# High-half products ahead of low-half products in every weight tile of a two-block fp32 network

## The reference

```
def reference(x, ...):
    x = first_block(x, ...)      # 2 layers: in-projection, mLSTM heads, retention heads, gates,
                                 # out-projection, feed-forward 1024-4096-1024, gated embedding
    return second_block(x, ...)  # layer 0: GLA + RWKV mixer, layer 1: attention with an index;
                                 # behind each a product-key expert layer with 16384 experts
...
z = h @ w_in[i] + b_in[i]
x = x + jnp.square(jax.nn.relu(h2 @ w_ff1[i] + b_ff1[i])) @ w_ff2[i] + b_ff2[i]
```

## Time and profile before

| what | value |
|---|---|
| median of 3 runs | 3336.14 us (3334.34 to 3337.27) |
| profiled execution, its own time | 3334.71 us |
| its span, first to last instruction | 3332.9 us |
| TensorE busy | 3222.9 us (97%) |
| VectorE busy | 2154.8 us (65%) |
| ScalarE busy | 1498.9 us (45%) |
| GpSimd busy | 506.1 us (15%) |
| DMA, mean | 170 GB/s |
| mean granted TensorE clock | 0.993 |

### The profile page before, as it was taken

How to read it: one execution, slowest core, us unless ns; L and a number is a source line. 1 busy time by engine, 2 the same in 40 slices (tenths; PEclk the granted TensorE clock), 3 DMA queues, 4 the chain that set the end, 5 groups by cost and what they waited for, 6 DMA issues and landing times.

```text
span 3332.9 us, 49471 instructions
## 1 busy us (share of the span) xinstructions
PE 3222.9 (97%) x20642; PEld 2851.4 (86%) x20642; DVE 2154.8 (65%) x3111; ACT 1498.9 (45%) x1717; POOL 506.1 (15%) x278
## 2 busy tenths in 40 slices
PE   8999999999999999989999999999999999999998
PEld 7787789787877897877999989888769999989887
DVE  6765665577666555685887755555677967655555
ACT  6444454564444544612444444444344444444443
POOL 0000000000000000010766600000003766300000
PEclk9999999999999999999999999999999999999999
DMA  5454645444545454303444465555424444565553
GB/s 222 149 184 165 214 165 188 166 152 163 182 169 207 173 183 166 146 18 112 175 167 149 152 234 199 189 189 193 173 89 152 166 164 152 198 220 182 197 190 126
DMA packets 87656, 565.12 MB, mean 170 GB/s; under 512 B 10192, under 2 KB 10208, under 8 KB 23568
## 3 DMA queue, kind: packets, MB, share of 16 engines
q1 hardware_dynamic: 80496, 534.81, 44.8%
q0 software_dynamic: 6944, 27.21, 2.5%
HBM read 552.54 MB, written 9.44 MB: 169 GB/s over the span
## 4 chain that ended last, share of the span: by engine, by line
PE 52%; DVE 5%; ACT 2%; issue 1%; POOL 1%; DVEq 0%; ACTq 0%
PE bank L1981 7%; PE bank L1982 7%; PE bank L1983 7%; PE bank L2004 7%; PE bank L2003 7%; PE bank L2002 7%; PE bank L1964 3%; ACT w_hi L2128 1%; PE bank L1713 1%; PE bank L1689 1%; PE bank L1691 1%; PE bank L1690 1%; PE bank L1715 1%; PE bank L1714 1%; POOL w_lo L1613 1%
## 5 line engine op out<-in xcount | busy, mean ns | idle before, releaser
L2128 ACT ACTIVATE w_hi<-raw 128x2048 fp32r<-128x2048 f32 x291 | 557.5, 1916 | 763.8 <-PE bank L2004 377.2
L2405 DVE TENSOR_TENSOR w_lo<-raw,w_hi 128x2048 fp32r<-128x2048 f32 x222 | 509.7, 2297 | 564.3 <-ACT w_hi L2128 563.6
L974 DVE TENSOR_TENSOR w_lo<-raw,w_hi 128x2048 fp32r<-128x2048 f32 x200 | 458.1, 2292 | 358.8 <-ACT w_hi L735 357.3
L735 ACT ACTIVATE w_hi<-raw 128x2048 fp32r<-128x2048 f32 x201 | 384.6, 1915 | 483.9 <-PE bank L489 330.7
L1981 PE MATMUL bank<-act_hi,w_hi 128*128 128x256 f32 x2048 | 591.9, 289 | 5.1 <-POOL w_lo L1613 5.1
L1983 PE MATMUL bank<-act_hi,w_lo 128*128 128x256 f32 x2048 | 580.2, 283 | 0.0
L1982 PE MATMUL bank<-act_lo,w_hi 128*128 128x256 f32 x2048 | 580.0, 283 | 0.0
L2004 PE MATMUL bank<-w_hi,c_lo 128*128 128x512 f32 x1024 | 399.5, 390 | 0.0
L2003 PE MATMUL bank<-w_lo,c_hi 128*128 128x512 f32 x1024 | 399.2, 390 | 0.0
L2002 PE MATMUL bank<-w_hi,c_hi 128*128 128x512 f32 x1024 | 399.0, 390 | 0.0
L1981 PEld LDWEIGHTS bank<-act_hi,w_hi 128*128 128x128 f32 x2048 | 392.9, 192 | 6.5 <-POOL w_lo L1613 6.3
(11 more groups left out here) (507 smaller groups left out, 5693.4 us busy)
## 6 DMA issues: line engine op xcount, KB each, us to landing
raw<-weights SPq DMA_DIRECT2D x492, 1024.0 KB, 4.8
row<-rows POOLq DMA_DIRECT2D x48, 256.0 KB, 4.3
spill<-staged SPq DMA_DIRECT2D x32, 256.0 KB, 2.9
hid<-spill SPq DMA_DIRECT2D x32, 256.0 KB, 4.8
y<-w_pe POOLq DMA_DIRECT2D x2, 1024.0 KB, 5.0
ln_row_mix<-ln_rows POOLq DMA_DIRECT2D x4, 512.0 KB, 4.9
hid<-keys POOLq DMA_DIRECT2D x2, 1024.0 KB, 6.2
ln_row_ffn<-ln_rows POOLq DMA_DIRECT2D x4, 512.0 KB, 7.7
```

What stands on the lines that cost most here:

```text
L735: nc.scalar.activation(w_hi[:, k % SPLIT, :], raw[:, k % RAW, :], ACT.Copy).then_inc(hi_ready, 1)
L974: nc.vector.tensor_tensor(w_lo[:, k % SPLIT, :], raw[:, k % RAW, :], w_hi[:, k % SPLIT, :].bitcast(F32), ALU.subtract).then_inc(lo_ready, 1)
L2128: A.activation(hi_of(k), raw[:, k % RAW, :], ACT.Copy).then_inc(hi_ready, 1)
L2405: V.tensor_tensor(lo_of(k), raw[:, k % RAW, :], hi_of(k).bitcast(F32), ALU.subtract).then_inc(lo_ready, 1)
```

## The change

In every weight tile TensorE waits for `hi_ready` first, issues all products with `w_hi` (high x high and low x high), then waits for the low half, and issues the products with `w_lo`. The number of products, their operands, and the place of `tile_used` at the tile's end stay. In the token-half form each half has its own high group and low group. In `hidden`, `gates` is called behind the same counts of products as before. The waits for activations (`ready`, `halves_of`) stand in the high group.

```
@@ first block, TensorE @@
+            def mm2(dst, lh, ll, rh, first):
+                nc.tensor.matmul(dst, lh, rh, start=first, stop=False)
+                nc.tensor.matmul(dst, ll, rh, start=False, stop=False)
...
             def natural(...):
                 for j in range(per) if tiles is None else tiles:
                     k = k0 + j
-                    pe.wait_ge(lo_ready, base + (k + 1))
+                    pe.wait_ge(hi_ready, base + (k + 1))
                     apart = half is not None and j == per - 1
-                    for kk, t in [... t outer] if apart else [... kk outer]:
-                        ...
-                        last = mm3(psum[2 * (c % 2) + t][:, :], hi[:, ki, ts], lo[:, ki, ts], w_hi[:, k % SPLIT, ws],
-                                   w_lo[:, k % SPLIT, ws], ki == 0, ki == per * KB - 1)
-                        if apart and t == 0 and kk == KB - 1:
+                    for group in [(t,) for t in range(TT)] if apart else [tuple(range(TT))]:
+                        for kk in range(KB):
+                            ki, ws = j * KB + kk, slice(kk * CW, (kk + 1) * CW)
+                            if ready is not None and 0 in group:
+                                ready(j, kk)
+                            for t in group:
+                                ts = slice(t * P, (t + 1) * P)
+                                mm2(psum[2 * (c % 2) + t][:, :], hi[:, ki, ts], lo[:, ki, ts], w_hi[:, k % SPLIT, ws], ki == 0)
+                        pe.wait_ge(lo_ready, base + (k + 1))
+                        for kk in range(KB):
+                            ki, ws = j * KB + kk, slice(kk * CW, (kk + 1) * CW)
+                            for t in group:
+                                last = nc.tensor.matmul(psum[2 * (c % 2) + t][:, :], hi[:, ki, t * P:(t + 1) * P], w_lo[:, k % SPLIT, ws],
+                                                        start=False, stop=ki == per * KB - 1)
+                        if apart and 0 in group:
                             last.then_inc(half, 1)
                     last.then_inc(tile_used, 1)
...
             def featured(...):   # both blocks alike; order is (f, kk) or (kk, f) in the first
-                    pe.wait_ge(lo_ready, base + (k + 1))
+                    pe.wait_ge(hi_ready, base + (k + 1))
+                    for kk, f in order:
+                        ...      # ready(j, kk) where f == 0, then w_hi x act_hi and w_hi x act_lo
+                    pe.wait_ge(lo_ready, base + (k + 1))
+                    for kk, f in order:
+                        ...      # w_lo x act_hi
                     last.then_inc(tile_used, 1)
@@ second block, hidden @@
-                wait_lo(pe, k)
+                pe.wait_ge(hi_ready, k + 1)
...
+                def product(of, jj, by, **marks):
+                    nonlocal done
+                    ws = slice((2 * kk_ + jj) * P, (2 * kk_ + jj + 1) * P)
+                    ins = mm(psum[4 + p % 2][:, jj * S:(jj + 1) * S], of[:, ws], by[:, kk_, :], **marks)
+                    done += 1
+                    if done == 3 * UNITS:
+                        ins.then_inc(tile_used, 1)
+                    if done % 3 == 0 and done // 3 - 1 in after:
+                        gates(after[done // 3 - 1])
                 for jj in range(2):
                     for kk_ in range(KD):
+                        product(wh, jj, act_hi, start=kk_ == 0 and jj == 0, stop=False)
+                        product(wh, jj, act_lo, start=False, stop=False)
+                wait_lo(pe, k)
+                for jj in range(2):
+                    for kk_ in range(KD):
+                        product(wl, jj, act_hi, start=False, stop=kk_ == KD - 1 and jj == 1)
@@ second block, output @@
-                wait_lo(pe, k)
+                pe.wait_ge(hi_ready, k + 1)
                 pe.wait_ge(c_lo_ready, p0 + o + 1)
+                for group in [(t,) for t in range(TT)] if end else [tuple(range(TT))]:
+                    parts = [(t, jj, c) for t in group for jj in range(2) for c in range(2)]
+                    ...          # for each part: c_hi x wh, c_lo x wh
+                    wait_lo(pe, k)
+                    ...          # for each part: c_hi x wl
```

More of the change, by code:

```diff
@@ L1680, in natural @@
                 k = k0 + j
-                wait_lo(pe, k)
+                pe.wait_ge(hi_ready, k + 1)
                 apart = half is not None and j == 1
[L1683 to L1692, removed]
+                for group in [(t,) for t in range(TT)] if apart else [tuple(range(TT))]:
+                    for kk_ in range(KB):
+                        ki, ws = j * KB + kk_, slice(kk_ * CW, (kk_ + 1) * CW)
+                        if 0 in group:
+                            halves_of(ki, split)
+                        for t in group:
+                            dst = psum[2 * (c % 2) + t][:, :]
+                            mm(dst, act_hi[:, ki, HALVES[t]], w_hi[:, k % SPLIT, ws], start=ki == 0, stop=False)
+                            mm(dst, act_lo[:, ki, HALVES[t]], w_hi[:, k % SPLIT, ws], start=False, stop=False)
+                    wait_lo(pe, k)
+                    for kk_ in range(KB):
+                        ki, ws = j * KB + kk_, slice(kk_ * CW, (kk_ + 1) * CW)
+                        for t in group:
+                            last = mm(psum[2 * (c % 2) + t][:, :], act_hi[:, ki, HALVES[t]], w_lo[:, k % SPLIT, ws], start=False, stop=ki == KD - 1)
+                    if apart and 0 in group:
                         last.then_inc(half, 1)
@@ L1710, in featured @@
                         dst = psum[2 * (c % 2) + f // 2][:, (f % 2) * S:(f % 2 + 1) * S]
[L1711 to L1715, removed]
+                        mm(dst, w_hi[:, k % SPLIT, ws], act_hi[:, ki, :], start=ki == 0 and f % 2 == 0, stop=False)
+                        mm(dst, w_hi[:, k % SPLIT, ws], act_lo[:, ki, :], start=False, stop=False)
+                wait_lo(pe, k)
+                for f in range(4):
+                    for kk_ in range(KB):
+                        ki = j * KB + kk_
+                        ws = slice(kk_ * CW + f * P, kk_ * CW + (f + 1) * P)
+                        dst = psum[2 * (c % 2) + f // 2][:, (f % 2) * S:(f % 2 + 1) * S]
+                        last = mm(dst, w_lo[:, k % SPLIT, ws], act_hi[:, ki, :], start=False, stop=ki == KD - 1 and f % 2 == 1)
                 last.then_inc(tile_used, 1)
@@ L1976, in hidden @@
                 after = dict(GROUPS_IN.get(p, ()))
+                done = 0
+                def product(of, jj, by, **marks):
[7 more added lines that the diff above has]
+                        gates(after[done // 3 - 1])
                 for jj in range(2):
-                    dst = psum[4 + p % 2][:, jj * S:(jj + 1) * S]
                     for kk_ in range(KD):
[L1980 to L1988, removed]
+                        product(wh, jj, act_hi, start=kk_ == 0 and jj == 0, stop=False)
+                        product(wh, jj, act_lo, start=False, stop=False)
+                wait_lo(pe, k)
+                for jj in range(2):
+                    for kk_ in range(KD):
+                        product(wl, jj, act_hi, start=False, stop=kk_ == KD - 1 and jj == 1)
             def output(o):
@@ L1993, in output @@
                 begin, end = o == 0, o == EXPERT_PAIRS - 1
-                wait_lo(pe, k)
+                pe.wait_ge(hi_ready, k + 1)
                 pe.wait_ge(c_lo_ready, p0 + o + 1)
                 wh, wl = hi_of(k), lo_of(k)
[L1997 to L2005, removed]
+                for group in [(t,) for t in range(TT)] if end else [tuple(range(TT))]:
+                    parts = [(t, jj, c) for t in group for jj in range(2) for c in range(2)]
+                    for t, jj, c in parts:
+                        cs, ws = slice(jj * S + t * P, jj * S + (t + 1) * P), slice(jj * D + c * CW, jj * D + (c + 1) * CW)
+                        mm(psum[2 * t + c][:, :], c_hi[:, o % 2, cs], wh[:, ws], start=begin and jj == 0, stop=False)
+                        mm(psum[2 * t + c][:, :], c_lo[:, o % 2, cs], wh[:, ws], start=False, stop=False)
+                    wait_lo(pe, k)
+                    for t, jj, c in parts:
+                        cs, ws = slice(jj * S + t * P, jj * S + (t + 1) * P), slice(jj * D + c * CW, jj * D + (c + 1) * CW)
+                        last = mm(psum[2 * t + c][:, :], c_hi[:, o % 2, cs], wl[:, ws], start=False, stop=end and jj == 1)
+                    if end and 0 in group:
                         last.then_inc(half_done, 1)
```

20 lines of the change are left out of this document (7 added, 13 removed).

## The result

The kernel with the change takes 3316.01 us (median of 4 runs, 3314.81 to 3319.13) against 3336.7 us for the kernel before (4 runs, 3334.34 to 3341.45): ratio 0.9932, 95% interval 0.992 to 0.9945. It is faster by 0.7%, 20.7 us by the medians, where 22.2 us were forecast. The profiled execution took 3319.13 us, with a span of 3317.3 us.

A forecast was written before the change was run, and what follows sets the result against it. TensorE works for 97% of the span, so only its 110 us of idle time and what slows its stream can be won. 24.6 - 0.7 - 1.7 = 22.2 us less gives 3313.5 us, range 3304 to 3327.

The forecast's parts named there:

- How large one stall is: TensorE's waits for w_lo: each costs its idle time + 0.25 us, since the idle column understates it.
- Removed, the first block: First block: 17 stalls for w_lo give 16.0 us, five tile starts too short for the idle column 1.9 us.
- Not kept: Three stalls per first-block layer and one in the second block: 6.7 us, counted at nothing, as TensorE then waits for VectorE.
- rival 2: All is kept: VectorE's chains also begin earlier, 6.7 us on top, and the clock costs nothing: 3305.5 us; chance 0.08.
- GpSimd's w_lo, "they are kept": Expert stage, three stalls per layer: 6.7 us stay gained; the nearest chain, the selection, has 5.4 us slack against 3.4 gained.
- What it adds, a fulfilled wait and bank changes: Some 500 mid-tile waits taken as 0 (outer end 40 us); bank switches of 2272 low products taken 0 (bound 23 us).
- Fresh activations: Second block's feature-major chunks: activations still being split are consumed faster, 0.24 us new wait three times, 0.7 us lost.
- The clock: First block, transposes: longer second wait may bring a 3.4 us stretch at 1.2 GHz in both layers; 1.7 us lost.
- more than two stretches beyond those of before: Sign of being wrong: more than two stretches at 1.2 GHz beyond those of the kernel before.
- 1 (half of the first block's gain lost): VectorE's chains turn half of the first block's 17.9 us into longer waits: gain 13 us, 3323 us; chance 0.20.
- 3 (slower by the wait): Mid-tile wait breaks the overlap of weight loads and products, 0.08 us per tile, net +18 us: 3354 us; chance 0.05.
- 4 (nothing): Nothing measurable: the high half isn't really early, or the gain is given back where weights stream; chance 0.05.

The follow-up runs named there:

- c_after: The kernel after, unaltered, run again as the mark for the follow-up edits to VectorE's and GpSimd's work: 3315.28 us, ratio 0.9933 to the kernel before.
- e6_y: Kernel after with VectorE's gatings put ahead of low splits (one in the mLSTM section, two in retention), so y is ready sooner: 3306.79 us, ratio 0.9911.
- e5_sel: Kernel after with the low half of the expert layers' tile 24 written by VectorE behind the selection instead of by GpSimd: 3310.95 us, ratio 0.9922.
- e3_order: New order of products in every tile, but TensorE waits for the low half at the tile's top as in the kernel before: 3338.92 us, ratio 1.0004.
- e4_waits: Kernel after plus about 5600 more fulfilled waits, one behind every pair of high products: 3313.24 us, ratio 0.9923 to the kernel before.
- c_after2: The kernel after, unaltered, run once more as the mark in a later group: 3315.47 us, ratio 0.9929 to the kernel before.
- e1_first: Kernel before with the new order and late wait in the first block only: 3316.48 us, ratio 0.9933.
- e7_both: Kernel after with both VectorE's earlier gatings of y and tile 24's low half moved from GpSimd to VectorE: 3305.08 us, ratio 0.9901.

## Why the prediction was right, step by step

Where the time went is read from the starts of the 492 `w_hi` in the profiles of before and c_after, whose spans differ by 3332.9 - 3314.8 = 18.1 us:

| part | forecast us | found us |
|---|---|---|
| first block, stalls kept | -17.9 | -18.3 |
| GpSimd's w_lo, kept | -6.7 | -6.6 |
| seven stalls not kept (y, keys) | 0 | 0 |
| selection late, both layers | 0 | +4.0 |
| granted clock in the first block | +1.7 | +5.6 - 3.2 = +2.4 |
| fresh activations, and what is left over | +0.7 | +0.4 |

The last row is what closes the sum. It holds steps of 1 to 1.5 us of both signs, and the larger ones lie at the clock: near 1395 us 1.5 us are lost where the granted clock is 0.50 for 6.8 us in c_after (from 1370.2) and for 3.4 us in before (from 1386.5), near 1420 and 2475 us 1.1 and 1.5 us are won the other way round (6.8 us at 0.50 in before, 3.4 in c_after), and near 2512 us 1.5 us are lost beside 3.4 us at 0.50 (from 2493.2) that before lacks.

**How large one stall is: right.** At the boundary of the earlier trace rows the gain is 1.20 us where the column said 0.98 and idle + 0.25 says 1.23. GpSimd's three in the first expert layer gave 1.26, 0.87 and 1.21 us, 3.33 us in all, and those of the second 3.30, against the 3.36 counted.

**Removed, the first block: right.** The sum over both layers is 9.2 + 9.1 us. The smallest, among them the five too short for the idle column, gave 0.35 to 0.45 us each, against 0.38.

**Not kept: right.** At the two places of the earlier trace rows the waits for y grew from 1.88 to 2.84 us and from 0.64 to 2.45 us (2.4 had been worked out); the gain at 343 us (0.86) is given back at the next tile (0.85), and the like in the second layer. The one stall of the second block went the same way: it is gone at 2405 us (1.03 us idle in before), and the wait for VectorE's keys 8 us behind it grew from 1.01 to 2.29 us. e6_y shows the cause for y: with y earlier, that time can be had. So rival 2 was wrong for this kernel; with e6_y's order on VectorE 31.4 us were measured where rival 2 said 30.6.

**GpSimd's w_lo, "they are kept": wrong, the one step that failed.** The stalls went as counted (-6.6 us), but the slack was reckoned as if `sel` took as long as before: 5.4 us of slack against 3.4 us gained. I took the durations of the earlier trace rows as they stood. Part of the price was readable there: `sel` took 1.85 us for two products, where the shortest in the trace took 0.29 us, so the first had already waited for GpSimd. By then TensorE has gained the first two stalls (1.26 + 0.87 = 2.1 us), so `w_hi` of the next tile is there when GpSimd ends, GpSimd goes on without its 1.2 us break, and the second product too falls into a split: 4.56 us instead of 0.29. That makes `sel` 4.3 us late, with 3.3 us gained 7.6 us. The slack was a little more than counted, since only the products of the second token half waited: they are the last three of the six that start at 1733.23 in before, at about 1733.5, 5.7 us behind `sel`. That leaves 1.9 us, and TensorE waits 1.77. 2.0 us a layer are lost, 4.0 in all; e5_sel gets them back (2.0 us in each layer by position).

**What it adds, a fulfilled wait and bank changes: right, at 0.** The rows at 231.76 to 239.27, and e3_order and e4_waits.

**Fresh activations: 0.7 us not seen.** TensorE's three listed waits for act_lo there are 3.9 us before and after; one step of 0.2 us at 1560 us is of the size that was counted. Most of this term is not shown.

**The clock: the reason was wrong, and the size is not shown.** I expected up to two more stretches at the 1.2 GHz level, behind the longer waits for y. The kernel before has one behind a wait of 1.88 us. In c_after the waits there are 2.84 and 2.45 us, and what follows runs at 1.00:

```profile
155.00:160.00 5.00, 3.41 (x23) 3.13 (x24) 3.04 (x6) 1.92 (x3) 1.08 (x2) 1.00 0.85 244
...
352.00:356.00 4.00, 4.00 (x25) 3.52 (x24) 4.00 (x2) 2.74 (x2) 0.00 (x0) 1.00 0.18 34
```

In the profile of the kernel after, which is the same program, the same waits are followed by slower stretches:

```profile
156.00:166.00 10.00, 9.83 (x43) 8.02 (x44) 6.56 (x8) 6.03 (x7) 1.07 (x2) 0.83 0.43 146
...
352.00:356.00 4.00, 3.38 (x17) 3.38 (x18) 3.65 (x3) 3.91 (x3) 0.00 (x0) 0.57 0.14 57
```

So it varies from one execution to the next, and the trace of before could not have "agreed" with the rule on idle time by two places. What c_after loses to the clock it loses elsewhere: in the stretches 28 to 40, 624 to 640 and 675 to 695 us (1.6 to 2.3 us each, 5.6 in all), while 3.2 us come back near 157 and 810 us. The profiles with the new first block differ in the places too: the stretch at 626 us is in both of c_after and c_after2 and not in e1_first or e4_waits. The sign that the prediction named, more than two stretches beyond those of before, did appear: ahead of the last 40 us before has 41.0 us at the 1.2 GHz level, c_after 51.2 and after 58.0. But the profile of before is a favourable one. The mean granted clock of each execution is known: 49 executions of before have 0.988 to 0.994, on average 0.9907, and the profiled one 0.993; 15 of the kernel after have 0.990 to 0.992, on average 0.9913. By these averages the clock takes 31 us from the kernel before and 29 from the kernel after, so over many executions no run shows the 1.7 us that the sum took off for it.

**The sum: 22.2 us forecast.** By the spans of these two profiles it is 18.1 us, 4.1 short, and 4.0 of that is the selection. The medians of the three groups with the unchanged kernel after give 20.7, 22.9 and 24.1 us; the profiled execution of before (3334.7 us) lies 2.0 to 4.9 us below the medians of its kernel in these groups. The forecast gain lies in the middle of the three, and that is partly luck: the selection, counted at nothing, took 4.0 us, and of the 2.4 us taken off for the clock and fresh activations hardly anything is seen over many executions. The working also gives 3336.1 - 22.2 = 3313.9 us where the prediction says 3313.5.

**Rivals.** 1 (half of the first block's gain lost): no, 18.3 us came where 17.9 were counted. 2 (all kept): not without e6_y's edits. 3 (slower by the wait): ended by e4_waits, 24.2 us faster than before with some 6100 waits in mid-tile. 4 (nothing): ended by the interval.

## What to carry to other kernels

Let an engine wait for each operand where it is first needed; a fulfilled semaphore wait between two products cost nothing that 5600 of them could show, so the order can be cut as fine as the producers are. Count a removed stall only when the next event that the engine waits for depends on the engine itself, and for every other chain work out its lateness anew, with the durations that its small instructions have when they fall beside other engines' long ones. Where a gain ends in a longer wait for another engine, reorder that engine next: here that gave nearly half as much again as the change itself (e7_both, 3305.08 us against 3315.28).

## What the runs showed of the hardware that was not expected

- A small VectorE operation can last as long as a GpSimd one beside it. The four `sel` products of 128x128 took 1541 ns at the least, 3052 at the median and 4560 at the most in the kernel after, and 291, 917 and 1547 ns in e5_sel:

```profile
L2829 DVE TENSOR_TENSOR sel<-best,gsum x4: 1541/3052/4560, 1713.5 to 2664.7; 128x128 f32<-128x128 f32 x4
```
```profile
L2829 DVE TENSOR_TENSOR sel<-best,gsum x4: 291/917/1547, 1708.0 to 2656.7; 128x128 f32<-128x128 f32 x4
```

- It goes the other way too: GpSimd's w_lo, 4.63 us at the median, takes up to 6.73 us. The one at 1708.16 started 0.06 us behind VectorE's L2773 of 2.29 us (two inputs), and is longer by 2.10 us:

```profile
L1626 POOL TENSOR_TENSOR w_lo<-raw,w_hi x70: 4500/4627/6730, 1475.5 to 2853.1; 128x2048 fp32r<-128x2048 f32 x70
```

 The Trainium skill (SBUF — State Buffer, "Who interferes with whom") says that a VectorE instruction with two SBUF inputs contends with a GpSimd one that reads SBUF, and that the second to issue blocks fully until the first has ended. The durations agree: 4.56 us for `sel` behind GpSimd, 4.63 + 2.1 us for GpSimd behind VectorE. VectorE's L2771, with one of its two inputs in a bank (PSUM), took its usual 2.29 us at 1705.78 while GpSimd was at work. By this rule the failed step could have been priced from the earlier trace rows.
- The granted clock behind a wait follows from neither the wait's length nor the program: behind the same wait of 2.8 us one execution of one program shows 1.00 and another 0.83 over 10 us, and behind a wait of 1.88 us the kernel before shows 0.50 over 3.4 us. In three profiles of the kernel after the time at the 1.2 GHz level, without the last 40 us, is 51.2, 51.2 and 58.0 us, so two executions of one program differed by 3.4 us (half of 6.8) for that alone; over all 14 profiles it is 41.0 to 58.0.
